# Chained layers: the first normalisation folded behind its products, the state-space table's steps moved to later places, and layer 1's scalar chain moved

## The reference

```python
# layer 0
h = rms_norm(x, even_norm_g); q, k, v, z_a, u, z_b = split(h @ even_w_in)
q, k = rms_norm per head (8 heads of 128)
o_a = stick_breaking_attention(q, k, v) * silu(z_a)
o_b = s5_mixer(u, ...) * silu(z_b)        # 32 groups, 64 complex states, then gelu and a gated product (GLU)
x = x + concat(o_a, o_b) @ even_w_out
# layer 1
h = rms_norm(x, odd_norm_g); q, k, v, z, r = split(h @ odd_w_in)
log_a = log_sigmoid(r @ gla_w_gate + gla_b_gate) / 16
o = gla_chunked(q, k, v, log_a)           # gated linear attention in chunks of 64
x = x + (rms_norm(o) * silu(z)) @ odd_w_out
# layers 2 and 3: dilated window attention and retention, merged; then a last rmsnorm
```

## Time and profile before

| | us |
|---|---|
| median of 3 runs (lowest and highest) | 1038.4 (1038.34 to 1040.05) |
| the profiled execution | 1038.45 |
| its span | 1036.6 |
| PE busy | 1003.6 (97%) |
| DVE busy | 699.9 (68%) |
| ACT busy | 553.6 (53%) |
| POOL busy | 199.5 (19%) |

### The profile page before, as it was taken

How to read it: one execution, slowest core, us unless ns; L and a number is a source line. 1 busy time by engine, 2 the same in 40 slices (tenths; PEclk the granted TensorE clock), 3 DMA queues, 4 the chain that set the end, 5 groups by cost and what they waited for, 6 DMA issues and landing times.

```text
span 1036.6 us, 15019 instructions
## 1 busy us (share of the span) xinstructions
PE 1003.6 (97%) x5948; PEld 881.3 (85%) x5948; DVE 699.9 (68%) x1098; ACT 553.6 (53%) x837; POOL 199.5 (19%) x206
## 2 busy tenths in 40 slices
PE   6899999998999999999999999999999999999996
PEld 5678889886978789998899888868999889988884
DVE  7984946977659756667766686674445556658666
ACT  6668577667436654455443354555444545334543
POOL 5800070010000006423213100010665000410000
PEclk9999999999999999999999999999999999999998
DMA  8543443767736499886666456546777456554551
GB/s 267 171 136 102 143 122 110 252 210 250 241 121 190 147 306 317 285 263 191 202 168 188 136 153 192 184 141 200 235 237 217 121 150 185 173 157 147 183 182 41
DMA packets 95350, 192.15 MB, mean 185 GB/s; under 512 B 8576, under 2 KB 11904, under 8 KB 95280
## 3 DMA queue, kind: packets, MB, share of 16 engines
q1 hardware_dynamic: 91440, 179.53, 56.0%
q0 software_dynamic: 3408, 11.18, 3.2%
q10 hardware_dynamic: 432, 0.49, 0.1%
HBM read 189.59 MB, written 1.05 MB: 184 GB/s over the span
## 4 chain that ended last, share of the span: by engine, by line
PE 88%; DVE 8%; ACT 2%; issue 1%; DMA 0%; POOL 0%; ACTq 0%; DVEq 0%
PE G L646 15%; PE G L648 14%; PE G L647 14%; PE G L655 9%; PE G L657 9%; PE G L658 9%; DVE WL L1638 2%; PE B L609 2%; PE B L979 1%; PE G L688 1%; PE G L690 1%; PE G L689 1%; PE B L959 1%; PE B L789 1%; PE B L969 1%
## 5 line engine op out<-in xcount | busy, mean ns | idle before, releaser
L1638 DVE TENSOR_TENSOR WL<-RAW,WH 128x1024 fp32r<-128x1024 f32 (+2 forms) x294 | 369.9, 1260 | 244.8 <-ACT WH L1107 243.8
L1107 ACT ACTIVATE WH<-RAW 128x1024 fp32r<-128x1024 f32 (+2 forms) x294 | 308.1, 1049 | 278.4 <-PE G L648 138.1
L646 PE MATMUL G<-WH,HTh 128*128 128x512 f32 (+2 forms) x556 | 225.0, 405 | 9.3 <-DVE WL L1638 9.2
L655 PE MATMUL G<-HTh,WH 128*128 128x256 f32 x768 | 219.2, 285 | 0.5 <-DVE WL L1638 0.3
L658 PE MATMUL G<-HTh,WL 128*128 128x256 f32 x768 | 217.3, 283 | 0.0
L657 PE MATMUL G<-HTl,WH 128*128 128x256 f32 x768 | 217.3, 283 | 0.0
L648 PE MATMUL G<-WL,HTh 128*128 128x512 f32 (+2 forms) x556 | 215.2, 387 | 0.0
L647 PE MATMUL G<-WH,HTl 128*128 128x512 f32 (+2 forms) x556 | 214.4, 386 | 0.0
L655 PEld LDWEIGHTS G<-HTh,WH 128*128 128x128 f32 x768 | 146.9, 191 | 2.5 <-issue 1.8
L657 PEld LDWEIGHTS G<-HTl,WH 128*128 128x128 f32 x768 | 146.9, 191 | 0.7 <-issue 0.5
L658 PEld LDWEIGHTS G<-HTh,WL 128*128 128x128 f32 x768 | 146.9, 191 | 0.0
(11 more groups left out here) (365 smaller groups left out, 1318.4 us busy)
## 6 DMA issues: line engine op xcount, KB each, us to landing
RAW<-in_w_in SPq DMA_DIRECT2D x176, 512.0 KB, 3.9
RAW<-in_even_w_in SPq DMA_DIRECT2D x40, 512.0 KB, 3.7
AR<-in_w_ada_t SPq DMA_DIRECT2D x32, 512.0 KB, 4.7
RAW<-in_odd_w_in SPq DMA_DIRECT2D x16, 512.0 KB, 4.4
AR<-in_w_ada_g POOLq DMA_DIRECT2D x32, 256.0 KB, 4.2
RAW<-in_w_proj_ret SPq DMA_DIRECT2D x16, 512.0 KB, 4.3
RAW<-in_w_out SPq DMA_DIRECT2D x16, 512.0 KB, 3.5
RAW<-in_even_w_out SPq DMA_DIRECT2D x12, 512.0 KB, 3.9
```

Of the source, the lines that this page charges most:

```text
L646: nc.tensor.matmul(o, xh, wh, start=begins, stop=False)
L655: nc.tensor.matmul(o, fh, h_[:, kx, :], start=begins and f % 2 == 0, stop=False, skip_group_check=True)
L1107: return nc.scalar.activation(out_, ps, ACT.Copy, **kw)
L1638: vt(wl, raw, wh.bitcast(F32), ALU.subtract).then_inc(*dve.mark(LO, n))
```

## The change

1. **Layer 0 joins the unscaled layers.** PE transposes X itself. The factor 1/rms of a token (NR) is applied where a product leaves its bank: as the scale of ACT's operations where tokens are on partitions (head sums, v, za by HR, which is half of NR), and by a tile RB where they lie along the columns (u and zb, whose evacuation DVE does now). RB is made by `factor_row`: ones times a diagonal of NR, a product of 128 by 256 in fp32 behind half 4, copied by ACT. rstd is computed once for both halves of the tokens, behind lo(2). `scaled` goes from DVE and POOL.
2. **The very beginning.** ACT's first instruction is a load of the function table; CI is asked for ahead of the columns. Half 0 of the tokens is turned whole before half 1. POOL clears its blocks first and asks for s_b, s_c, positions and masks when hi(0) is done. SP asks for RAW 0 between the two halves of X.
3. **Places.** The numbers of AT_S5 and its neighbours; `PARTS_FIRST` names times at which hi and lo go ahead of the other work of that time; u's 16 spreading transfers are asked for four at a time; in layer 0's end o0b is cut in two groups (o0b, o0e) and glu stands later.
4. **Layer 1.** `rstd` and `rows` at zr + 4 instead of + 2, the scan's tail in `gla_rest` two halves later, decay at 127, lo(n0 + 2) ahead of two HTl groups, and WGT, RES and GM asked for on SP.

The core of the diff:

```diff
-AT_S5 = {"powers": 1, "cos": 3, "lp": 4, "factor": 7, "c": 9, "in_re": 12, "in_im": 15, "out_re": 18, "out_im": 21,
-         "heads": (24, 49), "table": {23: 0, 26: 1, 27: 2, 28: 3, 29: 4, 30: 5},
+AT_S5 = {"powers": 1, "cos": 3, "lp": 4, "factor": 8, "c": 10, "in_re": 12, "in_im": 18, "out_re": 22, "out_im": 32,
+         "heads": (26, 50), "table": {34: 0, 35: 1, 36: 2, 38: 3, 40: 4, 43: 5},
...
-         "near_out": (32, 34), "turn": (35, 37, 38, 39), "in": (40, 42, 45, 47), "scan": (52, 54),
+         "near_out": (33, 37), "turn": (40, 42, 43, 44), "in": (45, 47, 49, 51), "scan": (55, 57),
...
-AT_SB_TURN = {70: ((0, 0),), 71: ((0, 2),), 81: ((1, 0),), 82: ((1, 2),)}
-AT_GELU = {"square": 72, "cube": 73, "tanh": 75, "y": 76, "hi": 80, "lo": 81}
-AT_GLU = 84
-AT_GLU_OUT = (89, 90)
+AT_SB_TURN = {70: ((0, 0),), 74: ((0, 2),), 81: ((1, 0),), 82: ((1, 2),)}
+AT_GELU = {"square": 75, "cube": 76, "tanh": 78, "y": 79, "hi": 84, "lo": 85}
+AT_GLU = 92
+PARTS_FIRST = (tuple(range(1, 40)) + (127, 155, 157), tuple(range(3, 40)) + (123, 125, 155, 157))
+AT_GLU_OUT = (97, 98)
...
-UNSCALED = (1,)
+UNSCALED = (0, 1)
...
+            def factor_row():
+
+                ps = take(("rb",), R_A.of("row"))
+                pe.wait_ge(*R_V.of("diagonal"))
+                nc.tensor.matmul(ps[:, 0:256], ONES, RD, start=True, stop=True).then_inc(*told("rb"))
...
-                        silu_half(name, SZB[:, ti, :], gbank(name, ti)[:, :], ti)
+                        act.wait_ge(*ZB_V.of(ti))
+                        nc.scalar.activation(SZB[:, ti, :], ZS[:, ti, :], ACT.Tanh, scale=0.5).then_inc(*act.mark(TH, name, ti))
...
-            for ti in range(2):
-                rstd(0, ti)
-                scaled(0, ti)
+            for r in range(4):
+                turned(0, 0, r)
             lo(0)
...
+            for r in range(4):
+                turned(0, 1, r)
+            lo(1)
+            lo(2)
+            rstd(0, slice(0, 2))
+            rows(0)
...
-                if time == 2 * groups["zr"]["at"] + 2:
+                if time not in PARTS_FIRST[1]:
+                    for n in made.get(time, ()):
+                        lo(n)
+                if time == 2 * groups["zr"]["at"] + 4:
                     rstd(1, slice(0, 2))
                     rows(1)
+                if time == AT_GLA["scan"] + 2:
+                    gla_rest()
```

More of the change, by code:

```diff
@@ L476, in program @@
         L2, H4 = range(2), range(4)
-        ROWS = events("rows", [1])
+        ROWS = events("rows", [0, 1])
         SUMSQ = events("sumsq", [(0, 0), (0, 1)] + [(l, ti, n) for l in range(1, 5) for ti in L2 for n in L2])
[L480 to L484, removed]
+        RSTD = events("rstd", [(l, ti) for l in range(5) for ti in L2 if l > 1 or ti])
+        HN_V, HN_A = (events(f"hn_{e}", [(l, ti) for l in (2, 3) for ti in L2]) for e in "va")
+        R_V, R_A = events("r_v", ["diagonal"]), events("r_a", ["row"])
+        TURNS = ([(0, ti, r) for ti in L2 for r in H4]
                  + [(1, ti, 2 * q + r) for q in L2 for ti in L2 for r in L2]
@@ L1021, in mrg_turn @@
                     *told("yt", "mrg", l, c))
-            for q in range(2):
-                for ti in range(2):
+            for ti in range(2):
+                for q in range(2):
                     norm_turn(0, ti, q)
@@ L1031, in tensor_program @@
                 half(time)
+                if time == AT_ROW:
+                    factor_row()
                 if time in AT_TURN1:
@@ L1101, in gbank @@
             return G[groups[name]["into"][ti]]
-        ENDS = {2 * last_of(n) + 1: n for n in groups if n not in ("o0c", "o0d") and n[0] != "close"}
+        ENDS = {2 * last_of(n) + 1: n for n in groups if n not in ("o0c", "o0d", "o0e") and n[0] != "close"}
         def scalar_program():
@@ L1485, in scalar_program @@
             for time in range(2 * groups["zr"]["at"] - 6):
+                if time in PARTS_FIRST[0]:
+                    for n in made.get(time, ()):
+                        hi(n)
                 if time in ENDS:
                     evac0(ENDS[time])
+                if time == AT_ROW:
+                    act.wait_ge(*side("rb"))
+                    copy(RB, bank_of["rb",][:, 0:256]).then_inc(*act.mark(R_A, "row"))
                 if time == 1:
@@ L1536, in scalar_program @@
                         *act.mark(YT_HI, "glu", 2 * i))
-                for n in made.get(time, ()):
-                    hi(n)
+                if time not in PARTS_FIRST[0]:
+                    for n in made.get(time, ()):
+                        hi(n)
             next_layer(1)
             for time in range(2 * groups["zr"]["at"], 2 * H0[0] - 6):
+                if time in PARTS_FIRST[0]:
+                    for n in made.get(time, ()):
+                        hi(n)
                 if time in ENDS:
@@ L1563, in scalar_program @@
                     yt_hi_scaled(YTh, 2 * h, lambda j: go[:, j:j + 1], "gla", h)
-                for n in made.get(time, ()):
+                for n in () if time in PARTS_FIRST[0] else made.get(time, ()):
                     if n in held:
@@ L1719, in rows @@
                     vt(R2, NR[1], NR[1], ALU.mult)
+                else:
+                    for ti in range(2):
+                        ins = ts(RD[:, 128 * ti:128 * ti + 128], IDENT, NR[0][:, ti:ti + 1], None, ALU.mult)
+                    ins.then_inc(*dve.mark(R_V, "diagonal"))
                 ts(HR[l], NR[l], 0.5, None, ALU.mult).then_inc(*dve.mark(ROWS, l))
@@ L2295, in vector_program @@
             for time in range(2 * groups["zr"]["at"] - 6):
+                if time in PARTS_FIRST[1]:
+                    for n in made.get(time, ()):
+                        lo(n)
                 if time in ENDS:
@@ L2350, in vector_program @@
                     dot(0, AT_DOT0.index(time))
-                for n in made.get(time, ()):
-                    lo(n)
+                if time not in PARTS_FIRST[1]:
+                    for n in made.get(time, ()):
+                        lo(n)
             next_layer(1)
@@ L2560, in rotate @@
                 gtt(o[:, 1, :], a[:, 1, :], b[:, 0, :], ALU.add).then_inc(*pool.mark(ROT, kind, l, i, ti))
-            nc.gpsimd.dma_start(BR, t["s5_b"]).then_inc(l_br, 16)
-            for ti in range(2):
-                scaled(0, ti)
-            pool.wait_ge(*HN_V.of(0, 1))
             for r in range(2):
```

137 lines of the change are left out of this document (72 added, 65 removed).

## The result

| | before | changed |
|---|---|---|
| median of 4 runs (lowest and highest) | 1039.22 (1038.34 to 1040.16) | 1049.05 (1045.93 to 1052.83) |
| ratio, 95% interval | 1 | 1.0092 (1.0064 to 1.0119) |
| the profiled execution / its span | 1038.45 / 1036.6 | 1048.68 / 1046.9 |
| PE busy | 1003.6 | 1011.3 |

The time lies outside the stated range (1031.5 to 1041.0). Two things stand out ahead of any row: PE is not only idle for longer but also *busy* for 7.7 us more, with one small product more to do, and the four runs of the changed kernel lie 7 us apart, those of the kernel before 2.

A forecast was written before the change was run, and what follows sets the result against it. Time was taken as PE's work (88% of the chain) plus moments when PE stands still. 1038.45 − 2.7 + 6.4 − 1.1 + 1.4 + 0.1 − 4.4 = 1038.2 us; range 1031.5 to 1041.0.

The forecast's parts named there:

- opening, to half 27: Layer 0's start: first weight product 1.6 us earlier, the stretch behind it 0.5 to 1.4 shorter; together −2.7 us.
- T: Moment ACT begins the HTh copies: 6.9 us taken; 6.4 if the table load holds no requests, otherwise 7.3 or 8.2.
- s5_turns: State-space table transposes at halves 40 to 44: PE waits for ACT's copies of M2, +6.4 us.
- sb_turn: sb_turn (0,2) moved from half 71 to 74, past the bank ACT emptied late: −1.1 us.
- piece 42: Half 84: lo(42) stands behind zb's DVE, ACT, DVE chain and four GELU operations; +1.4 us, between 0 and 2.2.
- closing pieces: Layer 0's end: the glu group's new place costs at most 0.2 us; +0.1 taken.
- layer 1: Of 4.8 us of PE waits from 60 to 420 us, 4.4 go by reordering; −4.4 us.
- behind it: Layers 2 and 3, taken as untouched by the change: no term in the sum.
- rival 4: A drain behind each ACT table load makes the s5_turn wait 1.4 us longer, total 1039.6; chance 3 in 100.
- Rival 1: Copies of M2 come in time, so no s5_turn wait: 1031.8 us; chance 0.38 with what lies between.
- rival 2: The opening wins nothing, as small delays at piece 3 eat the 2.7 us: 1040.9, slower; chance 0.13.
- The requests on SP: Layer 1: SP's three requests stand ahead of one weight piece with over 1 us to spare; no cost.

The follow-up runs named there:

- e4: Changed kernel plus 14 products of a zero block on PE just before the third s5_turn takes its banks; 1053.39 us, ratio 1.0122.
- e12: Kernel before with only layer 1's part of the change and sb_turn (0,2) at half 74 instead of 71, timed again; 1033.96 us, ratio 0.9951.
- e2: Changed kernel with hi(42) and lo(42) ahead of the other work of time 79; 1044.92 us, ratio 1.0052.
- e7: Changed kernel with the places of the state-space table, head transposes and GELU put back as before; 1039.84 us, ratio 1.0.
- experiment 3: Changed kernel with two and three added 256-column products on PE behind the opening's two groups of transposes; 1047.46 us, ratio 1.008.
- e1: Changed kernel with the near copies at 32 and 34 and the four s5_turns at 35, 37, 38, 39 as before; 1046.3 us, ratio 1.0064.
- e8: The run of experiment 3: changed kernel with five added 256-column products on PE before its first weight product; 1047.46 us, ratio 1.008.
- e6: Kernel before with only layer 1's part of the change and sb_turn (0,2) at half 74 instead of 71; 1033.61 us, ratio 0.9945.
- e3: Changed kernel with s5_turns and near copies put back and hi(42), lo(42) ahead of the other work of time 79; 1041.97 us, ratio 1.0045.

## Why the prediction was wrong, step by step

| step of the prediction | forecast | profile | what it was |
|---|---|---|---|
| opening, to half 27 | −2.7 | −1.6 | T right, the rest given back |
| (no step) a dip at 62 us | 0 | +1.6 | clock |
| s5_turns | +6.4 | +9.1 | waits 7.9 (at full clock, e4), clock 1.2 |
| sb_turn | −1.1 | −1.3 | |
| piece 42 | +1.4 | +5.2 | wait 3.5, clock 1.6 |
| closing pieces | +0.1 | +0.7 | pieces 49 to 51 |
| layer 1 | −4.4 | −3.7 | a wait at 82 for one at 80 |
| behind it | 0 | +0.3 | piece 197 |
| sum, of spans | −0.3 | +10.3 | the spans differ by 10.2 |

**The clock has no term in the sum.** This is the largest part, 4.4 of 10.6 us. The prediction read in one profile of the kernel before that the clock was full throughout, and took it as full after the change too, whatever PE would wait. A wait of 5 us was priced at 5 us. The traces show 1.2 to 1.6 more behind each of the two long ones. The third part, 1.6 at 62 us, came with PE at work. It is no property of the change: e12 has the same dip on the old opening, and the kernel before has runs 1.6 us longer at a lower mean clock. One execution in the faster of these groups was the base of the sum.

**The wait at `s5_turn` was found, and sized too small.** The fourth mask was to end 13.6 us behind half 31 and the copies to be done at 26.1 to 27.1; measured 13.7 (87.78, half 31's work ending at 74.09) and 27.4 (101.5). The 13.6 came out right although the terms listed for it add up to 11.5 only; in the trace the rest is DVE's wait of 2.4 for a high part, up to 83.77. ACT's part:

```profile
L1256 ACT ACTIVATE TK<-G,SM 128x128 f32<-128x128 f32 x8 | 2.8, 377 | 0.0
...
L1296 ACT ACTIVATE AR<-AR 128x768 f32<-128x768 f32 x2 | 1.7, 847 | 1.4 <-DVE AR L2087 1.4
L1302 ACT ACTIVATE AR<-AR 128x768 f32<-128x768 f32 x2 | 1.6, 898 | 0.0
...
L1299 ACT ACT_TABLE_LOAD x1 | 1.3, 1283 | 0.0
```

These are groups of ACT from 87 to 102 us. The squares take 2.8 where they took 2.1: the scale from a column costs 0.09 each, the upper bound of the step. Nothing stands idle behind the load, so rival 4 is out: the drain that the Trainium skill's page "ScalarE: Activation LUTs" (What ACT_TABLE_LOAD costs) puts behind each load is not seen here either. The wait is 6.4, not 4.6 to 6.2. The second wait, forecast as 0.5 to 1.2 at half 44, does not stand in the changed kernel's own waits, as PE's slower work covered it; in e4, at full clock, it is 0.8, with 0.3 more at the turn ahead of it. Rival 1 (the copies come in time), which held 0.38, rested on "before, no wait stands there". Before, the copies stood elsewhere in ACT's order, and that should have counted for nothing.

**Piece 42** is the term that was mis-sized most. DVE from 191 to 201 us:

```profile
191.78 1.22 DVE L1660 TENSOR_TENSOR WL<-RAW,WH 128x1024 fp32r<-128x1024 f32 x1
192.91 1.22 DVE L2381 SCALAR_TENSOR_TENSOR CB<-AR,CB 128x1024 f32<-128x1024 f32 x1
194.05 0.69 DVE L1894 TENSOR_TENSOR AR<-G,RB 128x512 f32<-128x512 f32 x1
195.44 0.69 DVE L1826 SCALAR_TENSOR_TENSOR AR<-AR 128x512 f32<-128x512 f32 x1 [0.70 <-ACT AR L1277]
...
200.16 1.22 DVE L1660 TENSOR_TENSOR WL<-RAW,WH 128x1024 fp32r<-128x1024 f32 x1
```

The prediction had 7.4, or 8.6 with the product with CB, from the end of zb to the end of lo(42). It was 9.7 (191.67 to 201.4): DVE still had lo(41) ahead of it when zb ended, which put both 1.1 us and CB in the way. It counted the chain from the moment its input was there and not from the moment DVE was free. PE's 6.4 us of cover was right (198.1), the wait 3.5. That it is the place in the order is shown by e2 and e7: with lo(42) ahead of the chain this wait is gone, and with four GELU operations less ahead of it, it is 1.4.

**The opening.** T was 6.29 (forecast 6.4 for the case that the load does not hold the requests, which it did not: it ran at 0.74 and CI was asked for at 0.78; 6.9 was taken), the first weight product at 11.41 (T + 5.1), lo(3) ended at 20.9 (T + 14.6, forecast 15.3). The steps up to there hold. (The 3.5 that the prediction gives for T = 6.4 does not follow from its own terms: 0.5 earlier than 6.9 makes it 3.2.) What failed is the sum of a start 1.6 earlier and a stretch 0.5 to 1.4 shorter: the first is not additive, since from piece 4 on PE waits for the low parts whatever its start (experiment 3). It was rival 2 (the opening wins nothing) up to piece 6; the 1.6 that remains comes at pieces 12 and 13, where out_im no longer stands.

**Layer 1** held, with three waits gone, but the silu set behind lo(80) pushed YTl behind piece 82; the prediction did not ask what the moved silu would be ahead of next. And lo(56) ahead of HTl moved 0.4 of wait to 0.6. The requests on SP held no weight piece up, but the prediction asked only what they would delay, not when they would come. The one for WGT went out at 246.46 and took 5.0 to land, 0.1 ahead of the product that needs it (251.6); before, GpSimd had asked at 230.51. In e1, e2 and e8 PE waited 0.6, 0.4 and 0.4 for it.

What stays open: why the clock dips at 62 us with PE at work. It does so in the profiles of the changed kernel, of e4 (for 13.7 us) and of e12, not in the other nine (e6 is e12's own program), at the same place in the program (the 32-column products of the near block and the half behind), and in others elsewhere. That the runs without a profile differ by such dips rests on their mean granted clock; where in the program they had them is not shown. Neither is how much of the clock that the changed kernel lost in its other runs came from its waits and how much would have come anyway. Also not taken apart is what of the changed opening makes DVE 3 us late at piece 12 in e7; a kernel with the new places on the old opening was not run.

## What to carry to other kernels

Before a step is moved, list what stands ahead of it on its engine in the new place, and start the clock of that queue when the engine is free, not when the data is there; both long waits were visible in the order alone. Two waits of TensorE of 6.4 and 3.5 us cost 1.2 to 1.6 more than their length here, so a change that shortens many small waits and makes a long one can be a bad trade. Compare the mean granted clock of two runs before their times: a difference of a thousandth was worth about 1 us in these kernels. And when PE is bound by helpers a few pieces later, an earlier start is worth nothing: test a gain at the next piece that waits. The parts of a change should be timed apart: the two that stood alone here are worth 0.55% by themselves (1033.6), and the rest cost 1.5%.

## What the runs showed of the hardware

- The granted clock fell to 0.50 during a wait of 6.4 us, 4.6 us after PE had stopped in the changed kernel (95.2 to 99.8), 2.0 in e2 and 5.1 in e8, and came back 5.1 to 5.9 us after PE had begun again (101.57 to 106.65 in the changed kernel). At a wait of 3.5 us it fell 0.2 us before PE began again (e1) to 1.2 behind (e4), for 3.4 us. In the one profile with a filled wait it stayed at 1.00.
- A wait of 2.2 us was followed by a dip of 3.4 us in e1 (at 399.9 us) and by none in e2 and e3 (piece 43); waits of up to 2.0 us in the kernel before by none. Dips came with PE at work as well, of 3.4 us at 62 us (the changed kernel, e12) and of 13.7 us at 63 us (e4).
- The first weight products at 11.4 us started 0.21 us apart until 14.5 us (until 17.5 in e1), at a granted clock of 1.00 in the profile's rows, and 0.12 apart when five products of 256 columns in fp32 stood ahead of them. With the old opening, at 13.4 to 13.6 us, they started 0.12 apart from the second on in two profiles of five.
- A table load at the start of ACT's program did not hold the DMA requests behind it (0.74 to 2.02 for the load, requests at 0.78 and 1.20).
- A scale read from a column made ACT's 128x128 squares 0.09 us longer each from start to start (0.34 instead of 0.25), and the whole of eight 0.7.
